# Local attention: ScalarE copies the transposes of three units ago ahead of the newest exponents

## The reference

```python
s = jnp.einsum('bnqgrd,bnkgd->bngrqk', qb, kk).astype(jnp.float32) * scale
s = jnp.where(mask[None, :, None, None], s, NEG_INF)
p = jax.nn.softmax(jnp.concatenate([s, sink], axis=-1), axis=-1)[..., :-1]
o = jnp.einsum('bngrqk,bnkgd->bnqgrd', p.astype(v.dtype), vv)
...
a = sliding_window_sink_attention(q, k, v, sinks).reshape(b, l, SWA_WIDTH) * jax.nn.silu(g_a)
c = jax.nn.silu(layer_norm(causal_depthwise_conv(u, conv_w, conv_b), ln_g, ln_b))
c = (c @ w_pw2) * jax.nn.silu(g_b)
return jnp.concatenate([a, c], axis=-1) @ w_out
```

## Time and profile before

| what | value |
|---|---|
| median of 3 runs | 2368.75 us (2362.07 to 2370.78) |
| the profiled execution | 2362.81 us, its span 2361.0 us |
| mean granted clock of TensorE | 0.962 |
| TensorE busy | 2210.5 us, 94% of the span |
| VectorE, ScalarE, GpSimd busy | 957.9, 786.7, 677.7 us |
| the stage, first scores to the last side matmuls | about 1815 to 1915 us after the span's start |

### The profile page before, as it was taken

One profiled execution on the slowest core, in us unless ns is written; L12 is line 12 of the kernel. 1 busy time (PEld: TensorE's weight loads), 2 busy tenths in 40 slices (PEclk: granted clock), 3 DMA queues, 4 the chain that ended last, 5 costly groups with the idle time before them and its releaser, 6 DMA issues.

```text
span 2361.0 us, 33133 instructions
## 1 busy us (share of the span) xinstructions
PE 2210.5 (94%) x13714; PEld 1869.2 (79%) x13714; DVE 957.9 (41%) x1306; ACT 786.7 (33%) x1261; POOL 677.7 (29%) x316
## 2 busy tenths in 40 slices
PE   4999989999999998999899999999999896999987
PEld 3787878888888887689887788888899685977766
DVE  3223143222222225653492422222689424066662
ACT  2212223122211122432594422322323533255542
POOL 0321323222222221323495344444120223300002
PEclk9999989999999998999899999999999897999998
DMA  7343213313232131231322233232222010211111
GB/s 283 134 160 135 81 45 137 114 63 142 98 113 91 54 134 45 72 68 60 61 29 73 81 98 95 91 98 90 72 81 81 10 52 30 81 54 56 56 46 41
DMA packets 74601, 200.96 MB, mean 85 GB/s; under 512 B 24688, under 2 KB 25968, under 8 KB 74480
## 3 DMA queue, kind: packets, MB, share of 16 engines
q1 hardware_dynamic: 73296, 198.63, 26.1%
q10 hardware_dynamic: 1184, 0.61, 0.1%
HBM read 195.54 MB, written 2.10 MB: 84 GB/s over the span
## 4 chain that ended last, share of the span: by engine, by line
PE 86%; DVE 5%; POOL 3%; ACT 2%; issue 2%; DMA 1%; SPq 0%; DVEq 0%; ACTq 0%; POOLq 0%
PE ps L1956 60%; PE ps L2077 5%; PE ps L2438 5%; PE ps L1971 3%; POOL NAP L852 2%; PE ps L2006 2%; PE ps L2140 1%; PE ps L1981 1%; PE ps L1995 1%; PE ps L2059 1%; PE ps L2462 1%; PE ps L2474 1%; PE ps L1988 1%; DVE S L1396 1%; DVE UC L1663 1%
## 5 line engine op out<-in xcount | busy, mean ns | idle before, releaser
L805 POOL TENSOR_TENSOR WL<-raw,WH 128x1024 fp32r<-128x1024 f32 x217 | 526.1, 2427 | 1421.1 <-ACT WH L902 1420.9
L902 ACT ACTIVATE WH<-raw 128x1024 fp32r<-128x1024 f32 x262 | 275.4, 1054 | 509.9 <-PE ps L1956 482.0
L1956 PE MATMUL ps<-HH,WH 128*128 128x512 f32 (+2 forms) x1568 | 427.5, 339 | 2.5 <-DVE HL L1765 2.5
L1956 PE MATMUL ps<-HH,WL 128*128 128x512 f32 (+2 forms) x1568 | 420.0, 334 | 0.0
L1956 PE MATMUL ps<-HL,WH 128*128 128x512 f32 (+2 forms) x1568 | 419.5, 334 | 0.0
L1956 PEld LDWEIGHTS ps<-HH,WH 128*128 128x128 f32 x1568 | 253.5, 189 | 62.6 <-issue 30.1
L1956 PEld LDWEIGHTS ps<-HL,WH 128*128 128x128 f32 x1568 | 252.6, 189 | 31.3 <-issue 1.4
L1956 PEld LDWEIGHTS ps<-HH,WL 128*128 128x128 f32 x1568 | 252.7, 189 | 30.9
L1956 PE MATMUL ps<-GL,WH 128*128 128x512 f32 (+1 forms) x896 | 267.0, 356 | 0.0
L1956 PE MATMUL ps<-GH,WL 128*128 128x512 f32 (+1 forms) x896 | 266.9, 356 | 0.0
L1956 PE MATMUL ps<-GH,WH 128*128 128x512 f32 (+1 forms) x896 | 266.3, 356 | 0.1
(11 more groups left out here) (259 smaller groups left out, 3309.9 us busy)
## 6 DMA issues: line engine op xcount, KB each, us to landing
raw<-stream SPq DMA_DIRECT2D x262, 512.0 KB, 3.6
ring<-stream SPq DMA_DIRECT2D x40, 1024.0 KB, 4.9
ADA<-stream SPq DMA_DIRECT2D x4, 2048.0 KB, 20.3
XT<-rpb SPq DMA_DIRECT2D x128, 24.0 KB, 2.3
XT<-xT SPq DMA_DIRECT2D x1, 2048.0 KB, 9.3
out<-XT SPq DMA_DIRECT2D x8, 256.0 KB, 2.0
V1s<-V SPq DMA_DIRECT2D x6, 256.0 KB, 4.6
XT<-ctxT SPq DMA_DIRECT2D x1, 1024.0 KB, 11.8
```

The source lines that it names most:

```text
L805: nc.gpsimd.tensor_tensor(WL[:, slot, :], raw[:, slot, :], WH[:, slot, :].bitcast(F32), ALU.subtract).then_inc(lo_done[slot], 1)
L902: nc.scalar.activation(WH[:, slot, :], raw[:, slot, :], ACT.Copy).then_inc(hi_done[slot], 1)
L1956: ins = nc.tensor.matmul(pair(g)[:, cols], lhs, x[:, k, cols], start=first, stop=last)
```

## The change

In ScalarE's loop the copy of unit k-3's transposes is issued ahead of the exponents of unit k, and not behind them. Nothing else differs: the same instructions, the same waits on each, and the streams of all the other engines are the same.

```diff
             for k in range(NU + 5):
+                if 3 <= k < NU + 3:
+                    sw_pt(k - 3)
                 if k < NU:
                     sw_exps(k)
-                if 3 <= k < NU + 3:
-                    sw_pt(k - 3)
                 if k == 2:
                     ahead(TILE["pw", 0])
                 if k == 7:
```

## The result

The changed kernel took 2371.34 us (median of 20 runs) against 2364.15 us for the kernel before (20 runs): ratio 1.0027, 95% interval 1.0021 to 1.0034. It is 0.27% slower, 6.4 us by the ratio and 7.2 us between the medians, clear of the noise, and inside the 0.5% that I had called no change. One run of the changed kernel took 6062.52 us and counts in no comparison. The profiled execution took 2368.91 us, with a span of 2367.1 us against 2361.0.

What follows compares the result with a forecast made beforehand. TensorE, with 86% of the last chain, was taken to bound the kernel. Terms 0 + 0.4 + 0.15 - 0.54 gave 0.0 us, so the forecast median was 2368.5 us, range 2360 to 2375.

Steps and rivals of the forecast that it cites:

- The ordinary step: In ordinary steps the copy runs earlier and the exponents 0.81 us later (0.5 in block 3), hidden by slack: 0.
- Step 4, the gain of 0: Unit 1's transposes start about 1.9 to 2.2 us earlier, but the layer norm matmuls still await convolution taps: gain 0.
- Step 4, the clock: A 2.2 us hole before the first layer norm group delays the clock's rise 0.8 us: +0.4 us, bounds 0 and +4.
- the 1841: Sign of a wrong prediction: half clock, expected to end near 1838, lasting until 1841 or longer.
- the clock comes back a good deal later: Rival at step 4: the clock's rise comes much later, +3.6 us, 2372 us; chance 0.2.
- Step 10, the exposed table load: The copy precedes the exponents' table load, so exponents start 2.08 us later and VectorE's reciprocal +0.15 us; bounds 0, +0.4.
- Step 17: Steps 16 and 17: unit 14's transposes no longer wait for the copy, -0.54 us; bounds 0 and -0.7.
- The sum: Whole kernel: ordinary 0, clock +0.4, table load +0.15, step 17 -0.54, giving 0.0 us; all bounds -0.7 to +3.9.
- The rivals that named table loads: Step 10's switch costs 1.28 us more, 2369.8 us, chance 0.02; three exposed loads, 3.9 of +15.9 us, chance 0.03.
- the exponents' delay in every step: Rival: delayed exponents are on every step's path, 12.0 us, plus exposed loads 3.9: +15.9, 2384.7 us; chance 0.03.
- TensorE keeps all it waited for: Rival: all three transpose waits for the copy, 3.9 us together, become gain: 2364.9 us; chance 0.06.

Runs made afterwards that it cites:

- second: Every copy but the first (step 3) moved ahead of the exponents, against the kernel before: ratio 0.9997, 2363.11 us.
- fourth experiment: The changed kernel with the old order in steps 10, 11 and 13, whose copies precede table loads; against the kernel before: ratio 1.0031, 2371.16 us.

## Why the prediction was wrong, by its own steps

**The ordinary step, 0: right.** With every copy but the first moved the ratio is 0.9997.

**Step 4, the gain of 0: right.** The wait went behind the product and became one for the taps, 2.16 us as the new hole, foreseen as 2.2.

**Step 4, the clock, +0.4 with an upper bound of +4: here the prediction failed.** The place and the cause were right, the size was not. The changed kernel lost 4.0 us by step 6 alone, which is the upper bound, and 1.6 and 2.7 more around steps 9 and 11, then 0.9 around step 13, from stretches that I had taken as unchanged. That is 9.2 us in the stage. The clock was back at 1848.1, which with the 0.40 taken off is far behind the 1841 that the prediction named as a sign of being wrong. Two choices were wrong. First, I took the delay of the rise, 3.1 us after the start of a group, from step 9's row, because it was the same operation behind a like pause. One row gives no such delay. The same group of step 9, behind a pause of 2.83 to 2.92 us and with full clock up to it, had the clock back 3.1 us after its start in the kernel before, 9.6 in the kernel with step 12's pause filled and 16.2 in the changed one. And the group of step 4, behind the same 2.16 us, had it back after 4.5 us in the kernel with one copy moved and after 12.6 in the changed one. A warning stood in the stretch itself: much TensorE work from 1822.7 on had not brought the clock back before 1837.4. Second, I bounded the loss at one step. A stage with a pause every few steps can fall again, and at step 9 it did: 17 us at half instead of 3. (The pieces that the bound names take 5.1 us at full clock, 1842.10 to 1847.23 in the trace before, and not 4; about 4 is what was left of such a step behind 1837.4.) I gave the rival "the clock comes back a good deal later" 0.2, at +3.6 us; this is the rival that came true, and its size should have been open above 4.

**Step 10, the exposed table load, +0.15: right in mechanism and size.** The kernel with all but the first copy moved runs its stage 0.67 us later at this place (its maximum stands at 1870.64, against 1869.97 before), and its rows are:

```profile
1868.21 0.81 ACT L1195 ACTIVATE S<-ps 128x768 f32<-128x768 f32 x1 [5.54 <-PE ps L2371]
...
1869.04 1.28 ACT L1179 ACT_TABLE_LOAD   x1
...
1870.33 0.49 ACT L1179 ACTIVATE SWP<-ps,SWs 128x273 f32<-128x273 f32 x1
...
1870.64 0.73 DVE L1750 TENSOR_REDUCE SWs<-ps 128x2 f32<-128x546 f32 x1 [1.76 <-PE ps L2351]
...
1871.41 0.17 DVE L1756 RECIPROCAL SWs<-SWs 128x2 f32<-128x2 f32 x1
```

Copy, load, exponents: 0.83 and 1.29 us apart, as computed. The reciprocal at 1871.41 - 0.67 = 1870.74 is 0.12 us later than in the earlier trace rows, and the gate behind it (1877.77, against 1876.89) 0.21 us. In the changed kernel this term does not show: TensorE's scores come so late there that the gate stands 6.92 us behind the maximum of step 11, as before. The drain of 1.38 us that the Trainium skill, page "ScalarE: Activation LUTs", section "What ACT_TABLE_LOAD costs", adds to a switch is not in these rows: the exponents start 1.29 us after the load's start, right behind a copy.

**Step 17, -0.54 with a bound of -0.7: right in mechanism, a little small.** In the same trace, 0.76 us late here:

```profile
1897.20 0.66 PE L2371 MATMUL ps<-con,SWP 128*128 128x128 f32 x4
...
1897.89 0.60 ACT L1195 ACTIVATE S<-ps 128x512 f32<-128x512 f32 x1 [2.20 <-PE ps L2371]
...
1900.01 0.60 PE L2371 MATMUL ps<-con,SWP 128*128 128x128 f32 x4
```

From the transposes of step 16 to those of step 17 it is 2.81 us, against 1899.92 - 1896.44 = 3.48 in the earlier trace rows: 0.67 us gained.

**The sum.** The +3.9 that the prediction gives for all bounds holds step 17's gain at -0.54; with its bound of 0 it is +4.4. With the measured sizes: 9.2 (clock, within the stage) - 0.7 = 8.5, the 8.5 us by which VectorE's last steps of the stage stand later (0.40 taken off). The span is 6.1 us longer, 5.7 without the 0.40. Of the other 2.8 us, 1.5 are given back right behind the stage, where the kernel before had a short fall of the clock (from 1915 to 1919) and the changed one had none. Over the end of the span another 1.6 are given back, as the clock fell at 2346.0 before and at 2356.7 in the changed execution; why is not known. In between, some tenths were lost. The rivals that named table loads (both of them) and the exponents' delay in every step are out by the second and fourth experiment. "TensorE keeps all it waited for" is out as well: all three waits are gone, and only the third gave anything, 0.67 us.

**Shown and not shown.** Shown: the first copy's move alone gives the loss; added matmuls in the pause take it away; a kernel with the old order and less work in that place has the same loss and the same stretches. That the loss is the clock's rests on this and on the traces, one for each kernel, whose times go with the sum of their stretches. Not settled: what decides in a single execution how long a stretch lasts, since the same group behind the same pause had the clock back after 4.5 or after 12.6 us, and why the stretch of step 9 lengthens together with the first. Not tried either: the same pauses with the whole stage moved a few microseconds against the program's start.

## What to carry to other kernels

When a change removes a wait on TensorE, look for where the idle time goes: if it gathers right ahead of a group that waits for something else, the idle time is the same and the clock may not be. Price a stretch at half clock over all the work that may fall into it, not from the quickest recovery in the trace, and expect it to be short in one execution and long in another behind the same pause. Where pauses of 1 to 3 us can't be avoided, matmuls without use in them are worth a trial: here 19 of them in five pauses made the kernel 0.30 to 0.35% faster, 4 to 5 us of medians.

## What the runs showed of the hardware that was not expected

Taking about 0.9 us of TensorE work out ahead of a wait made the kernel 0.31% slower (1.0019 to 1.0043); putting 1.25 us of useless work in ahead of the same wait took a loss of 0.27% away. And in the traces the state of the clock in one place goes with its state some 20 us later: the three executions with a first stretch of 27 us (the changed kernel, the one with the old order at the loads, the one with less work) had a second one of 17 us, all the others one of at most 10. The third stretch does not follow: it was 14 us in those three, and 24 us in three others whose first was short.
